# Combine rows and convolution taps as full 128x128 matmuls, with 8 instead of 16 taps on TensorE

## The reference

```python
def conv_mix(x, buf, ...):                      # causal, 31 taps, one filter per channel
    h = x @ w_pw1 + b_pw1
    u = h[..., :D] * sigmoid(h[..., D:])
    full = concatenate([buf, u], axis=1)
    c = depthwise_conv(full, w_dw) + b_dw       # c[t, d] = sum_k full[t + k, d] * w_dw[k, d]
    return silu(layernorm(c)) @ w_pw2 + b_pw2, full[:, -30:]

def peer(x, w_q, sub_keys, u_tab, v_tab):       # for each token and each of 8 heads
    q = x @ w_q                                 # two halves of 128
    s = einsum('bhpc,hpnc->bhpn', q, sub_keys)  # 2 x 128 scores
    idx, best_s = the 16 best of the 16 x 16 pairs of the best keys
    gate = softmax(best_s)
    act = gelu(einsum('bhkd,bd->bhk', u_tab[idx], x))
    return einsum('bhk,bhkd->bd', gate * act, v_tab[idx])
```

## Time and profile before

| | |
|---|---|
| runs | 3980.32 us median of 3 (3977.02 to 3980.86) |
| profiled execution | 3980.32 us, its span 3978.5 us |
| mean granted TensorE clock | 0.853 |
| busy over the span | PE 74%, DVE 69%, ACT 37%, POOL 36% |
| gathers | 1152, 1208 MB of the 1311 MB moved |
| phases of picks | 894 to 1556, 1556 to 2417, 2417 to 3140, 3140 to 3957 us |

### The profile page before, as it was taken

How to read it: one execution, slowest core, us unless ns; L and a number is a source line. 1 busy time by engine, 2 the same in 40 slices (tenths; PEclk the granted TensorE clock), 3 DMA queues, 4 the chain that set the end, 5 groups by cost and what they waited for, 6 DMA issues and landing times.

```text
span 3978.5 us, 56287 instructions
## 1 busy us (share of the span) xinstructions
PE 2955.1 (74%) x20248; PEld 1449.0 (36%) x20248; DVE 2732.4 (69%) x6352; ACT 1470.4 (37%) x4424; POOL 1424.2 (36%) x1272
## 2 busy tenths in 40 slices
PE   5999999868766666777777766788787676666655
PEld 3777777754222122333333322334342222222111
DVE  5555555546766666778777777889867677777775
ACT  1333333313433333444444433444444343333333
POOL 0001110014444444344444444334444444444442
PEclk8888999889787778888889888999998787787777
DMA  2110000039999999999999999999999999999996
GB/s 79 30 30 26 25 25 25 18 111 425 426 426 427 426 427 426 421 416 399 411 404 426 426 426 425 415 353 369 421 394 427 426 425 427 426 426 426 426 426 289
DMA packets 229640, 1311.06 MB, mean 330 GB/s; under 512 B 58736, under 2 KB 61936, under 8 KB 81648
## 3 DMA queue, kind: packets, MB, share of 16 engines
q0 software_dynamic: 165888, 1208.03, 72.6%
q1 hardware_dynamic: 63472, 99.43, 7.1%
HBM read 1301.52 MB, written 5.86 MB: 329 GB/s over the span
## 4 chain that ended last, share of the span: by engine, by line
DMA 36%; PE 19%; DVE 16%; ACT 3%; issue 3%; DVEq 1%; POOL 1%; ACTq 1%; POOLq 0%
DMA arena<-in_uv,arena 36%; DVE arena L1587 8%; PE psum L1159 8%; PE psum L1121 4%; PE psum L1211 3%; PE psum L1241 2%; DVE arena L1674 1%; POOL arena L1101 1%; ACT wbuf L1377 1%; PE psum L1231 1%; ACT arena L1372 1%; DVE arena L1515 1%; DVE arena L1512 0%; ACT arena L1368 0%; DVE arena L1648 0%
## 5 line engine op out<-in xcount | busy, mean ns | idle before, releaser
L1159 PE MATMUL psum<-arena,wbuf 64*64 64x512 f32 (+1 forms) x8704 | 1451.1, 741 | 865.7 <-ACT wbuf L1377 846.3
L1101 POOL DMA_INDIRECT arena<-in_uv,arena x1152 | 1349.7, 1172 | 1770.7 <-PE psum L1159 1569.4
L1587 DVE SCALAR_TENSOR_TENSOR arena<-arena 128x1024 f32<-128x1024 f32 x1152 | 1396.0, 1222 | 584.9 <-DMA arena<-in_uv,arena 569.6
L1159 PEld LDWEIGHTS psum<-arena,wbuf 64*64 64x64 f32 (+1 forms) x8704 | 335.0, 154 | 1755.5 <-ACT wbuf L1377 1379.3
L1368 ACT ACTIVATE arena<-arena 128x2 f32<-128x2 f32 x576 | 117.0, 203 | 1668.1 <-DVE arena L1587 1663.4
L1377 ACT ACTIVATE wbuf<-cst,arena 128x64 f32<-128x64 f32 x1152 | 338.3, 340 | 41.6 <-issue 2.4
L1121 PE MATMUL psum<-arena,wbuf 128*128 128x256 f32 (+1 forms) x1024 | 312.4, 453 | 8.5 <-DVE arena L1598 5.8
L1372 ACT ACTIVATE arena<-arena 128x1 f32<-128x1 f32 x1152 | 276.8, 287 | 40.9 <-issue 1.4
L1121 PEld LDWEIGHTS psum<-arena,wbuf 128*128 128x128 f32 x1024 | 203.9, 210 | 171.5 <-issue 131.2
L842 POOL COPY arena<-arena 128x256 f32<-128x256 f32 x8 | 3.2, 397 | 584.2 <-DVE arena L735 584.2
L406 PE MATMUL psum<-arena,wbuf 128*128 128x288 f32 x768 | 193.6, 411 | 0.4 <-DMA wbuf<-in_w_rkv 0.4
(11 more groups left out here) (264 smaller groups left out, 3322.9 us busy)
## 6 DMA issues: line engine op xcount, KB each, us to landing
wbuf<-in_w_q SPq DMA_DIRECT2D x64, 576.0 KB, 11.8
arena<-in_w_pw SPq DMA_DIRECT2D x48, 512.0 KB, 8.7
arena<-in_uv,arena POOLq DMA_INDIRECT x1152, 20.3
wbuf<-in_w_rkv SPq DMA_DIRECT2D x24, 512.0 KB, 3.6
wbuf<-in_w_o SPq DMA_DIRECT2D x8, 512.0 KB, 3.7
arena<-in_w_o SPq DMA_DIRECT2D x8, 512.0 KB, 8.5
x<-in_x SPq DMA_DIRECT2D x1, 2304.0 KB, 8.2
arena<-in_state SPq DMA_DIRECT2D x16, 128.0 KB, 3.0
```

The source lines that it names most:

```text
L1101: pool.indirect_dma_start(ring[:, g % RING, :], None, I["uv"][p // 2], bass.IndirectOffsetOnAxis(ap=idx[:, s % 4, j:j + 1], axis=0)).then_ ...
L1159: last = pe.matmul(ps[e * HD:(e + 1) * HD, 2 * (u % 2) + a if u < NB else 4, :], diag[t, g % DIAGS, :], ring[t, g % RING, D + e * 512:D + ...
L1587: stt(out=row, in0=row, scalar=1.0, in1=tok[p % 2][:, UNITS[p % 2].index(u), :], op0=ALU.mult, op1=ALU.mult, accum_out=dots[:, g % COLS:g ...
```

## The change

The diagonals become full 128x128 matrices from the full identity `K.ident`. A full unit's pick is then two matmuls of 128x128 by 512 columns, one for each half of the features, each with a bank of its own; the picks of unit 4 keep their two matmuls to 64 columns. PSUM so holds tokens on all 128 partitions and one half of the features a bank, and the flush on DVE adds one block of 512 columns where it added two of 256. The taps on PE become full diagonals too, and are 8 instead of 16; DVE does 23 instead of 15. PE and ACT spread their 8 taps over the same number of rows of the schedule as the 16 before. Both tables of diagonals together keep or double their room in SBUF (8 x 128 for 16 x 64, and 8 x 128 for 8 x 64).

```diff
-    PE_TAPS = 16
+    PE_TAPS = 8
...
-    diag = W.cut(DIAGS, HD)
+    diag = W.cut(DIAGS, P)
...
-    tap_diags = R.cut(PE_TAPS, HD)
+    tap_diags = R.cut(PE_TAPS, P)
...
-                for a in range(2 if u < NB else 1):
-                    t = slice(a * HD, a * HD + HD) if u < NB else slice(0, P)
-                    for e in range(2):
-                        last = pe.matmul(ps[e * HD:(e + 1) * HD, 2 * (u % 2) + a if u < NB else 4, :], diag[t, g % DIAGS, :],
-                                         ring[t, g % RING, D + e * 512:D + (e + 1) * 512],
-                                         start=head == 0 and j == 0, stop=head == HEADS - 1 and j == PICKS[u] - 1)
+                for e in range(2):
+                    out = ps[:, 2 * (u % 2) + e, :] if u < NB else ps[e * NS:(e + 1) * NS, 4, :]
+                    last = pe.matmul(out, diag[:, g % DIAGS, 0:P if u < NB else NS],
+                                     ring[:, g % RING, D + e * 512:D + (e + 1) * 512],
+                                     start=head == 0 and j == 0, stop=head == HEADS - 1 and j == PICKS[u] - 1)
...
-                        yield from tick.until(at + k // 8)
-                        for e in range(2):
-                            q = slice(e * HD, e * HD + HD)
-                            last = pe.matmul(part[q], tap_diags[q, k, :], ups[c % 2][q, k:k + 2 * P], start=k == 0, stop=k == PE_TAPS - 1)
+                        yield from tick.until(at + k // 4)
+                        last = pe.matmul(part, tap_diags[:, k, :], ups[c % 2][:, k:k + 2 * P], start=k == 0, stop=k == PE_TAPS - 1)
...
+                same = K.ident if u < NB else K.ident2
...
-                    act.activation(diag[:, (g + k) % DIAGS, :], K.ident2, ACT.Copy, scale=coef[:, c:c + 1]).then_inc(diag_ready, 1)
+                    act.activation(diag[:, (g + k) % DIAGS, 0:P if u < NB else NS], same, ACT.Copy,
+                                   scale=coef[:, c:c + 1]).then_inc(diag_ready, 1)
...
-                        yield from tick.until(t["project"] if c == 0 else at + 5 + k // 4)
+                        yield from tick.until(t["project"] if c == 0 else at + 5 + k // 2)
...
-                        last = act.activation(tap_diags[:, k, :], K.ident2, ACT.Copy, scale=K.par[:, TAP0 + k, c:c + 1])
+                        last = act.activation(tap_diags[:, k, :], K.ident, ACT.Copy, scale=K.par[:, TAP0 + k, c:c + 1])
...
-                        to = u * P + e * HD
-                        for k in range(2):
-                            dst = K.x[:, 4 * k:4 * k + 4, to:to + HD]
-                            last = tt(dst, dst, got[:, :, k * HD:(k + 1) * HD], ALU.add)
+                        if u < NB:
+                            dst = K.x[:, 4 * e:4 * e + 4, of_unit(u)[0]]
+                            last = tt(dst, dst, got, ALU.add)
+                        else:
+                            for k in range(2):
+                                dst = K.x[:, 4 * k:4 * k + 4, T:N]
+                                last = tt(dst, dst, got[:, :, k * NS:(k + 1) * NS], ALU.add)
```

More of the change, by code:

```diff
@@ L1361, in pair @@
             def pair(s, j):
+                u = SEQ[s][2]
                 g = START[s] + j
                 q = slice(g % COLS, g % COLS + 2)
+                same = K.ident if u < NB else K.ident2
                 if j == 0:
```

## The result

The changed kernel takes 4031.94 us (median of 4 runs, 4029.28 to 4032.52), the kernel before 3979.10 in the same comparison: ratio 1.0130, 95% interval 1.0115 to 1.0145, so 52.8 us slower. The prediction was 4063 (+83), with a range of 4008 to 4150. The profiled execution of the changed kernel took 4034.49 us, its span 4032.7.

What follows compares the result with a forecast made beforehand. The gather's DMA was taken to pace most of the retrieval, DVE the convolution of half B and PE its linear. Terms 38 + 13 + 19 + 6 + 5 + 2 = 83 us on 3980 gave 4063 us, range 4008 to 4150.

Steps and rivals of the forecast that it cites:

- A row, +0.82 us: Each full unit's combine row on PE: 1.84 us instead of 1.02, +840 us of PE in all at full clock.
- Convolution B, +38: Convolution of half B: DVE stays the limit, its added taps cost 33 us and added waits 5; bounds +16 and +55.
- the 5 us that I added for waits: Convolution of half B: 5 us more because DVE's fifth tick of a chunk waits for PE's first two.
- Convolution A, +13: Convolution of half A: DMA, PE and DVE nearly full, DVE's 32 us only partly fit into gather waits; bounds 0 and +35.
- Linear B, +19: Linear of half B: PE already the limit, 24 dearer rows show less 0.7 us of idle time; bounds 10 and 22.
- Linear A, +6: Linear of half A: 16 dearer full rows, partly covered by PE idle time and rows in flight; bounds 0 and 14.
- the start, +5: Linear at the start: 24 dearer rows, about 15 of 20 us taken from gathers in flight; bounds 0 and 17.
- the end, +2: End of the kernel: the last rows stand bare and cost 2 us.
- Light parts, 0: Light parts: a pick needs 2.12 us of PE in 2.5, so the dearer rows cost nothing.
- PE as the bound everywhere: Rival for the whole kernel: at the low clock PE binds everywhere, over 4140 us, about 4160; chance 0.17.
- Only the taps show: Rival: dearer rows are hidden and only DVE's +33 us in convolution B show, 4013 us; chance 0.10.
- The faster rival: Rival: DVE's tap waits vanish and rows cost nothing, linear B included, about 3970 us; chance 0.05.

Runs made afterwards that it cites:

- experiment 2: The kernel before with 8 instead of 16 taps on PE, rows and taps still in 64x64 quadrants: 4004.59 us, ratio 1.0067.
- experiment 1: The changed kernel with 16 taps on PE in quadrants, schedule and narrow diagonals as before: 4015.64 us, ratio 1.0098 against the kernel before.

## Why the prediction was right

The direction, the places and, but for the start, the order of the places were right; the sum was 30 us too large. Nearly every term was too large and the start alone a little too small, so it is not luck of errors that cancel. By its own steps:

- **A row, +0.82 us.** Measured 1.72 us from start to start, so +0.70. The 1.84 us that I took came from four groups of projection. In order of time these are one run of three groups (1839.89 to 1845.27, 5.38 us) and one group alone (1846.29 to 1848.21, 1.92 us), both with rows in quadrants on either side; less 0.2 us each they are 5.18 and 1.72, that is 1.72 to 1.73 a group. The 2.35 us that I used as upper bound holds the same 0.2. The row before of the earlier trace rows stands behind 2.00 us of idle time and not between two blocks, as I read it, but one between two blocks takes 1.02 us too (1845.27 to 1846.29). What I said of the drain, that my sum goes by spacings in which it is already contained, was the fault: contained meant counted, and after the change it is gone. This term, the price of a row and of the blocks beside it, is the one that was mis-sized. The rule of the Trainium skill that I set beside it (TensorEngine Tiling (Array Packing), Key Properties: changing the tiling mode drains the engine) was the better guide. The traces agree with it: 2.35 to 2.15 us for the same block, 3.66 to 3.45 for eight taps.
- **Convolution B, +38.** Measured +28.0. Step by step: 64 taps at 0.48 to 0.52 us, 31 to 33, came as +30.5 of DVE's busy time; the 5 us that I added for waits had the wrong sign, as DVE's waits for the tap sum and the gate fell from 18.5 to 11.7. PE was said to be 18 us behind DVE and not to show; experiment 2 gives the same 356 us without the dear rows. PE was in fact further behind than my sum of 329 us at full clock says: it was busy 318.3 us at 0.95, which is about 302 at full clock by the same estimate as above. The step holds; its size was 10 us too large.
- **Convolution A, +13.** Measured +4.8. The rows alone cost 9.5 (experiment 1), the taps alone −0.8 (experiment 2), and in both together, with PE's 8 taps fewer a chunk and one shape throughout, some 5 us of the rows' cost come back; the runs don't tell these two apart. I had the parts (DVE's taps fit into its waits for the gather, PE near its limit) and guessed the remainder too high.
- **Linear B, +19.** Measured +15.1. With the prices now known an estimate is 24 rows x 0.70 = 16.8, less 16 product blocks x 0.20 = 3.2, together 13.6; the 15.1 were read over 28 picks. What was missing is the drain once more.
- **Linear A, +6, the start, +5, the end, +2.** Measured +3.1 (picks 454 to 576) and +5.8 (0 to 256); from the last pick to the end it is 24.7 us in both traces, so nothing for the end. The stretch behind linear B (763 to 832), which had no term, gave back 2.0. At the start 12.9 us are lost in 32 picks and 7.1 regained. I had put this down to the gathers in flight, and the ring of 8 slots bears it out: there 11.4 are lost and none regained.
- **Light parts, 0.** Measured −0.1 in phase 3. The low clock, which carried the largest rival, did not stay: 0.94 in 3500:3700, where it was 0.81, with PE at 81% instead of 65. The rule of the Trainium skill cited for it (TensorE: Matmul & The Clock Gate, Part 1: activity releases the throttle) agrees with that row.

Of the rivals, PE as the bound everywhere fell with the clock. "Only the taps show" is right in convolution B and for the taps' own 29 us, and wrong in linear B and at the start, where the rows have another 20. The faster rival asked that rows be hidden in linear B and tap waits vanish; neither came. The two halves of the change are not additive, 40 and 29 us alone and 53 together, and the stretches say why: in convolution B the rows alone cost 8.7, the taps alone 28.3, and both 28.0, for the length goes by the busier of PE and DVE. As the limit of that stretch passes to PE when rows are dear and 16 taps stay on it, moving taps to DVE is what the dear rows invite; but moving all 8 makes convolution B 19 us longer than rows alone do (336.9 to 356.2) and returns only some 5 us in convolution A. Of the three kernels with full rows the one with all eight taps moved is the slowest: ratio 1.0098 with 16 taps on PE, 1.0096 with 12, 1.0130 with 8.

What stays open: why convolution B gains so little when DVE has less to do (5 us for 15). The waits point to PE's projections and taps, and with 20 taps neither PE (busy 278.9 of 323.1 us) nor DVE (274.5) is full, but no run here separates PE's speed from the order in which the chunk's steps wait for each other.

## What to carry to other kernels

Cost a change by stretch and ask in each which engine waits for nothing: the same 30 us of VectorE work were free beside a gather that bound and cost 28 us where VectorE was the limit, and some 700 us of added TensorE time (1024 rows at 0.70 us) cost about 40. The convolution of half B, nearly balanced between two engines, behaved as a ridge: work moved onto the fuller one showed in full, work moved off it by a third (5 us of 15). When a price is read from a row, ask what else that row holds, here the change of shape on both sides, and whether it is still there after the change.

## What the runs showed of the hardware

- Four 64x64 float32 matmuls of 512 columns in four quadrants take 1.02 us between full blocks, two rows of them 1.88; the same product as two full 128x128 matmuls takes 1.72. A diagonal matrix has two empty quadrants of four, and the full form, which has to cover them, takes 0.70 us more.
- A block of 128x128 matmuls between blocks of another shape takes about 0.2 us longer, 0.1 for each side: 2.35, 2.25 and 2.15 us for four matmuls of 320 columns with two, one and no such neighbour, 3.66 and 3.45 for eight taps with two and none.
- The granted clock over the whole span rose from 0.853 to 0.941 with PE's busy share from 74 to 85%, which gave back part of the added work: the row group's busy time grew by 645 us (1451.1 to 2096.5), where 1024 rows x 0.70 at full clock are 717. Two rows in quadrants took 2.92 and 3.69 us in the light part before (3504.50 and 3508.22, clock 0.64 over 3500:3512), and 1.95 at 1.00.
- With 11 or with 8 ring slots the gathers of 1 MB come at the same 2.55 us a pick in the light parts. The other three slots are a store from which a lag can be taken (7.1 us at the start), and without them the kernel before was 42 us slower, half of it in convolution A.
